# Unread TensorE products in the fox, mlstm and HGRN stages of a two-block kernel, and where these stages begin

## The chip, the cores and the metric

The kernel runs on one core of a Trainium2 chip. TensorE does the matrix products, VectorE, ScalarE and GpSimd the elementwise work, SyncE issues the transfers. The metric is the time of one execution on the device in microseconds; for the kernel before it is the median of three runs. TensorE's clock has two levels in this trace, and the profile gives the granted one as a share of the full 2.4 GHz: 1.00 or 0.50.

## What is computed

Two transformer blocks on 512 tokens of width 1024 in f32. The change touches the second one, whose four mixers (s5, HGRN, fox, mlstm, 256 columns each) stand between an input projection and an output projection. Cut to what matters, and for mlstm and HGRN in the form over all tokens in which the kernel computes them:

```python
# block 2, after block 1 (dilated and latent attention, then an MLP) on x [1, 512, 1024], all f32
qh, kh, vh = heads(q), heads(k), heads(v)              # fox: 4 heads of 64
s = q @ k.T * 64**-0.5 + F[:, None] - F[None, :]       # F = cumsum(log_sigmoid(fz))
s = where(k_pos <= q_pos, s, -1e30)
out = softmax(s) @ v                                   # then a norm by head

# mlstm: q, k = silu(causal 4-tap convolution), gates ig, lf; 4 heads of 64
qk = (q @ k.T) * exp(b[t] - b[s] + ig[s] - m[t]),  s <= t
h = (qk @ v) / max(|sum(qk)|, exp(-m[t]))

# HGRN2: per-channel decays b = cumsum(log f)
scores[t, s] = sum_k q[t,k] * k[s,k] * exp(b[t,k] - b[s,k]),  s <= t
o = scores @ v
# s5: a complex scan, then y = gelu(y) * sigmoid(gelu(y) @ w_glu)
# y = concat(s5, hgrn, fox, mlstm) @ w_out; residual; norm; gated MLP; residual
```

## The kernel before

Tokens lie in four tiles of 128. The program is a row of stages, each an `nc.Block()` with one instruction stream for each engine; a stage's end is a meeting of all engines. Within a stage the engines are ordered by counting semaphores alone, and each engine takes its own instructions in the order of the code. So what stands ahead of an instruction on its engine delays it, whatever it is. PSUM has eight banks, `k.pb[0]` to `k.pb[7]`.

**proj2** (`stage_proj2`) projects the second block's inputs and runs the s5 scan beside it. Its tail is `glu.products`: 24 products of 256 columns into banks 6 and 7, each quarter followed by a sigmoid on ScalarE (`gates`, semaphore `glu.gate`, four counts) and a scaling on VectorE (`scale`).

**fox** (`stage_fox`, which calls `stage_attention`) has 16 batches, four heads by four query tiles; batch i of a head has (i mod 4) + 1 key tiles. TensorE's loop over i runs the scores of batch i, the four or fewer transposes of the probabilities of batch i-1 (`turn`) and the products with the values of batch i-2 (`mix`, 64 columns each). The scores are an f32 product of 64 rows (two instructions in the trace), one of 4 rows for the decays, and a bf16 one with the identity that adds the mask. VectorE takes the maximum, ScalarE the exponential. `Convolution` puts mlstm's convolution on VectorE in iterations 0 to 3 and its sigmoids on ScalarE in iteration 5. The other two attention stages, of the first block, call the same function.

**mlstm** (`stage_mlstm`) also has 16 batches. `scores(b)` makes the logarithms of the decays (2 rows, and the mask) and the f32 scores; ScalarE takes the exponential, VectorE multiplies (`ml_pT`). `scores(b)` waits for the exponential and the product of batch b-2. After the four batches of a head, `mix` of the head before has 20 instructions of 65 columns. `HgrnGates` puts HGRN's gates on VectorE (batches 1, 5 and 10) and on ScalarE (batches 3 and 7).

**HGRN** (`stage_hgrn`) has ten levels (`halves`); at each, VectorE makes operands (`hg_z`, semaphore `zr`), TensorE runs four heads of products into banks 0 to 3, and VectorE selects from them (`sel`). Levels 8 and 9 need a new scan on VectorE. A second block mixes the result with the values while GpSimd and VectorE do the norms of the other mixers; after a third one comes `stage_turn` with transposes, and then the output projection.

Of the kernel before, what the change touches and what calls it, by code (L numbers as in the profile page):

```python
# [30 lines left out]
T = S // P  # L31
# [205 lines left out]
def products(k, out, pairs, first, last):  # L237

    n = 0
    for a, b in pairs:  # L240
        for x, y in ((a.hi, b.hi), (a.hi, b.lo), (a.lo, b.hi)):
            mm = k.nc.tensor.matmul(out, x, y, start=first and n == 0, stop=last and n == 3 * len(pairs) - 1)  # L242
            n += 1
    return mm


def note_freed(k, steps, done):
# [454 lines left out]
        self.free.base += len(self.steps)  # L702


def stage_attention(k, batches, scale, bufs_kb, lse=None, beside=None):

# [19 lines left out]
    with nc.Block() as block:  # L728
# [5 lines left out]
        @block.tensor  # L734
        def _(pe):
            def scores(i):
                b = batches[i]
                if i >= 2:

                    pe.wait_ge(expd.sem, expd.base + i - 1)  # L740
                for (c0, c1), parts in zip(b["segs"], b["scores"]):
                    for m, (a, r, lo, hi, *row) in enumerate(parts):

                        at = dict(tile_position=(row[0], 0)) if row else {}
                        mm = nc.tensor.matmul(k.pb[i % 2][:, lo:hi], a, r, start=m == 0,  # L745
                                              stop=m == len(parts) - 1, skip_group_check=True, **at)
                mm.then_inc(scored.sem, 1)

            def turn(i):
                b = batches[i]  # L750
                pe.wait_ge(expd.sem, expd.base + i + 1)
                if i >= 2:
                    ev = (ev_act, ev_dve)[i % 2]

                    pe.wait_ge(ev.sem, ev.base + i // 2)
                for c in range(0, width(b), P):
                    mm = nc.tensor.transpose(k.pb[2 + i % 2][:, c:c + P], probs[:, i % 2, c:c + P], k.ident[:, :])
                mm.then_inc(turned.sem, 1)

            def mix(i):  # L760
                b = batches[i]
                ev = (ev_act, ev_dve)[i % 2]
                pe.wait_ge(ev.sem, ev.base + i // 2 + 1)
                if i >= 2:

                    pe.wait_ge(out_free.sem, out_free.base + i - 1)
                for n, ((c0, c1), vs) in enumerate(zip(b["segs"], b["values"])):
                    for m, v in enumerate(vs):
                        mm = nc.tensor.matmul(k.pb[4 + i % 2][:, n * DH:(n + 1) * DH],
                                              probsT[:, i % 2, c0 + m * P:c0 + (m + 1) * P], v,  # L770
                                              start=m == 0, stop=m == len(vs) - 1, skip_group_check=True)
                mm.then_inc(mixed.sem, 1)

            for i in range(nb + 2):
                if i < nb:
                    scores(i)
                    if beside is not None:
                        beside.pe(pe, i)
                if 1 <= i <= nb:
                    turn(i - 1)  # L780
                if i >= 2:
                    mix(i - 2)
# [1097 lines left out]
def stage_proj2(k, g):  # L1880
# [15 lines left out]
    for name, _, a, b in PROJ2_FEATURES:  # L1896
        wide = b - a
        tiles = feature_tiles(k.xT, (0, P), wide) if wide == 256 else feature_tiles(k.xT, (0,), wide, m=wide)
        s, j, g = gemm(k, g, KD, 8, tiles, j, BANKS)
# [3 lines left out]
    for c in range(2):  # L1903
        s, j, g = gemm(k, g, KD, 4, token_tiles(lhs, [(0, 512, 0)], 512), j, BANKS)
        steps += s
    s, j, g = gemm(k, g, KD, 8, token_tiles(lhs, [(0, 256, 0)], 256), j, BANKS)
# [6 lines left out]
    rows, glu = GateRows(k), S5Glu(k, end)  # L1913
# [21 lines left out]
    with nc.Block() as block:  # L1935
# [7 lines left out]
        @block.tensor  # L1943
        def _(pe):
            def inject(n):
                q = 32 * (n % 4)
                if n == 0:
                    pe.wait_ge(copied.sem, copied.base + 2)
                else:

                    pe.wait_ge(taken.sem, taken.base + n)
                for c in range(2):
                    mm = nc.tensor.matmul(k.pb[4 + c][:, :], bT[q:q + 32, c, n // 4, :], uT[q:q + 32, n // 4, :],
                                          start=True, stop=True, tile_position=(q, 0))
                mm.then_inc(bu.sem, 1)

            def project(n):
                q = 32 * (n % 4)
                pe.wait_ge(prod.sem, prod.base + n + 1)
                nc.tensor.matmul(k.pb[6 + n // 4][q:q + 32, :], cT[:, 0, n, :], bufs[n % 2][:, 0, :], start=True,  # L1960
                                 stop=False, tile_position=(0, q), skip_group_check=True)
                nc.tensor.matmul(k.pb[6 + n // 4][q:q + 32, :], cT[:, 2, n, :], ei[:, n, :], start=False,
                                 stop=True, tile_position=(0, q), skip_group_check=True).then_inc(out_done.sem, 1)

            seen = set()
            for i, (c, j, out, pairs, start, last) in enumerate(steps):
                if c not in seen:
                    seen.add(c)
                    n = c - first - 2
                    if 0 <= n - 2 < 6:  # L1970
                        project(n - 2)
                    if 0 <= n < 8:
                        inject(n)
                    wait_chunk(k, pe, c)
                if (c, j) == (first + 9, j_tm + 1):
                    project(6)
                if (c, j) == (first + 10, j_tm + T + 2):
                    project(7)
                if (c, j) == (first + 11, j_tm + T + 2):
                    rows.turn(pe)  # L1980
                if j == j_tg + 2:
                    rows.read(pe)
                    glu.turn(pe)
                if start and j >= 4:

                    pe.wait_ge(copied.sem, copied.base + j - 3)
                mm = products(k, out, pairs, start, last)
                if last:
                    mm.then_inc(done.sem, 1)
                elif i in marks:  # L1990
                    mm.then_inc(k.w_used.sem, 1)
            glu.products(pe)

        @block.scalar
        def _(act):
# [318 lines left out]
def stage_fox(k):  # L2314

    batches = []
    for h in range(4):
        lo = DH * (h % 2)
        q, kk = k.fm[lo:lo + DH, 6 + h // 2, :], k.fm[lo:lo + DH, 8 + h // 2, :]
        for t in range(T):  # L2320
# [5 lines left out]
                         (k.identb[:, :], k.mask_row[:, :], t * P, w)]],  # L2326
                values=[[k.tm[:, 2, u, h * DH:(h + 1) * DH] for u in range(t + 1)]],
                out=k.ycat[:, t, 512 + h * DH:512 + (h + 1) * DH]))
    stage_attention(k, batches, 1.0, 158, beside=Convolution(k))


def stage_mlstm(k, hg):
# [12 lines left out]
    with nc.Block() as block:  # L2345
        @block.tensor
        def _(pe):
# [30 lines left out]
            for h in range(5):  # L2378
                if h < 4:
                    for u in range(T):  # L2380
                        scores(4 * h + u)
                if h >= 1:
                    mix(h - 1)

# [117 lines left out]
def stage_hgrn(k, hg):  # L2502
# [20 lines left out]
    with nc.Block() as block:  # L2523
# [81 lines left out]
        def _(pe):  # L2605
            for i in range(nl):
                if i >= 1:
                    pe.wait_ge(zr.sem, zr.base + i)
                for h in range(4):
                    m = 4 * i + h  # L2610
                    if m >= 4:
# [5 lines left out]
                    n = halves[i]  # L2617
# [321 lines left out]
```

## Time and profile before

| | us |
|---|---|
| median of 3 runs | 1773.5 (1773.2 to 1774.2) |
| the profiled execution | 1772.9, of which the span is 1771.1 |
| TensorE busy with products | 1619.4 (91%) |
| VectorE busy | 828.3 (47%) |
| ScalarE busy | 553.8 (31%) |
| mean granted clock of TensorE | 0.92 |
| fox | about 1139.6 to 1200.2 |
| mlstm | about 1200.6 to 1255.6 |
| HGRN, levels | about 1255.9 to 1302.7 |

The span runs from the first to the last instruction; all places in time are microseconds from its start. A line such as `L745` is the line of the code that issued an instruction, and `bank<-fm` says that it wrote a PSUM bank from the tile `fm`; `x4` merges four such instructions in a row. What stands in brackets behind is the engine's idle time before it and what ended that. "Busy" of TensorE is a union of modelled product times, so a busy stretch can hold less array work than it seems.

### The profile page before, as it was taken

How to read it: one execution, taken by the hardware profiler on the slowest of the kernel's cores; microseconds unless marked ns; L12 is line 12 of the kernel's file. 1: busy time of each engine (PE TensorE's matmuls, PEld its weight loads, DVE VectorE, ACT ScalarE, POOL GpSimd, SP SyncE). 2: the span in 40 equal slices, each digit the busy share in tenths (PEclk: the TensorE clock that was granted, in tenths of full speed). 3: DMA queues.
4: the chain of work that ended last, by engine and by line, in shares of the span. 5: the costliest groups of instructions: out<-in, count | busy, mean ns of one | idle time of the engine just before them, and what ended most of it. 6: DMA issues, size and time to landing. Idle time of an engine off the chain costs nothing. (4 is left out here: it accounts for less than half of the span.)

```text
span 1771.1 us, 18376 instructions
## 1 busy us (share of the span) xinstructions
PE 1619.4 (91%) x7372; PEld 1297.5 (73%) x7372; DVE 828.3 (47%) x1217; ACT 553.8 (31%) x839; POOL 261.3 (15%) x275
## 2 busy tenths in 40 slices
PE   7987999678988899999997999999868899999997
PEld 6875777566767788888886766765757688888886
DVE  4233333446654444434336666644664533323434
ACT  4221333424442432222224213334123422212222
POOL 0000000000020697000002466000320100000000
PEclk9999999889998999999998999855759899999999
DMA  4222111220022223222231222200002222222222
GB/s 163 96 92 74 48 48 60 72 72 1 1 71 84 75 102 102 102 97 95 95 119 33 95 72 72 79 0 1 1 1 71 72 95 95 95 95 95 97 85 92
DMA packets 34633, 129.23 MB, mean 73 GB/s; under 512 B 4548, under 2 KB 18780, under 8 KB 22132
## 3 DMA queue, kind: packets, MB, share of 16 engines
q1 hardware_dynamic: 34260, 127.93, 21.1%
q8 instruction: 58, 0.95, 0.2%
q14 instruction: 27, 0.22, 0.0%
q10 hardware_dynamic: 288, 0.12, 0.0%
HBM read 124.82 MB, written 3.17 MB: 72 GB/s over the span
## 5 line engine op out<-in xcount | busy, mean ns | idle before, releaser
L223 DVE TENSOR_TENSOR ring_lo<-ring_raw,ring_hi 128x2048 fp32r<-128x2048 f32 (+5 forms) x115 | 266.7, 2322 | 218.5 <-ACT ring_hi L213 218.4
L242 PE MATMUL bank<-xT_hi,ring_hi 128*128 128x512 f32 (+1 forms) x864 | 342.7, 397 | 5.1 <-PEq L1257 3.4
L242 PE MATMUL bank<-xT_hi,ring_lo 128*128 128x512 f32 (+1 forms) x864 | 338.8, 392 | 0.0
L242 PE MATMUL bank<-xT_lo,ring_hi 128*128 128x512 f32 (+1 forms) x864 | 338.8, 392 | 0.0
L213 ACT CAST ring_hi<-ring_raw 128x2048 fp32r<-128x2048 f32 (+5 forms) x115 | 212.7, 1852 | 270.4 <-DMA ring_raw<-in_w_ff 131.1
L242 PEld LDWEIGHTS bank<-xT_hi,ring_hi 128*128 128x128 f32 (+1 forms) x864 | 163.4, 189 | 44.6 <-issue 10.0
L242 PEld LDWEIGHTS bank<-xT_hi,ring_lo 128*128 128x128 f32 (+1 forms) x864 | 162.8, 188 | 35.6
L242 PEld LDWEIGHTS bank<-xT_lo,ring_hi 128*128 128x128 f32 (+1 forms) x864 | 163.1, 189 | 34.3
L242 PE MATMUL bank<-ring_hi,hid_hi 128*128 128x512 f32 x432 | 169.9, 393 | 4.0 <-DVE ring_lo L223 4.0
L242 PE MATMUL bank<-ring_lo,hid_hi 128*128 128x512 f32 x432 | 169.4, 392 | 0.0
L242 PE MATMUL bank<-ring_hi,hid_lo 128*128 128x512 f32 x432 | 169.3, 392 | 0.0
L1131 POOL TENSOR_TENSOR stat<-stat 128x1 f32<-128x1 f32 x28 | 18.2, 652 | 701.9 <-DVE stat L1172 701.9
L242 PE MATMUL bank<-ring_hi,xT_hi 128*128 128x512 f32 (+1 forms) x288 | 111.5, 387 | 8.9 <-DVE ring_lo L223 8.9
L242 PE MATMUL bank<-ring_hi,xT_lo 128*128 128x512 f32 (+1 forms) x288 | 110.2, 382 | 0.0
L242 PE MATMUL bank<-ring_lo,xT_hi 128*128 128x512 f32 (+1 forms) x288 | 110.1, 382 | 0.0
L242 PEld LDWEIGHTS bank<-ring_hi,hid_hi 128*128 128x128 f32 x432 | 82.1, 190 | 21.4 <-DVE ring_lo L223 4.4
L803 ACT ACTIVATE probs<-bank,nm 128x128 f32<-128x128 f32 (+3 forms) x96 | 50.2, 527 | 148.9 <-DVE nm L829 148.8
L242 PEld LDWEIGHTS bank<-ring_lo,hid_hi 128*128 128x128 f32 x432 | 82.0, 190 | 17.1
L242 PEld LDWEIGHTS bank<-ring_hi,hid_lo 128*128 128x128 f32 x432 | 81.9, 190 | 17.2
L242 PEld LDWEIGHTS bank<-ring_hi,xT_hi 128*128 128x128 f32 x288 | 58.9, 204 | 21.7 <-DVE ring_lo L223 6.5
L827 DVE TENSOR_REDUCE mx<-bank 128x1 f32<-128x512 f32 (+4 forms) x72 | 43.3, 601 | 54.3 <-PE bank L745 54.3
L242 PEld LDWEIGHTS bank<-ring_hi,xT_lo 128*128 128x128 f32 x288 | 58.8, 204 | 9.1
(440 smaller groups left out, 2297.4 us busy)
## 6 DMA issues: line engine op xcount, KB each, us to landing
ring_raw<-in_w_ff SPq DMA_DIRECT2D x32, 1024.0 KB, 4.8
ring_raw<-in_w_up SPq DMA_DIRECT2D x22, 1024.0 KB, 4.9
ring_raw<-in_w_proj SPq DMA_DIRECT2D x8, 1024.0 KB, 5.2
ring_raw<-in_w_gates SPq DMA_DIRECT2D x8, 1024.0 KB, 4.9
ring_raw<-in_w_out SPq DMA_DIRECT2D x8, 1024.0 KB, 4.9
ring_raw<-in_w_fm SPq DMA_DIRECT2D x12, 512.0 KB, 4.5
ring_raw<-in_w_dn_a SPq DMA_DIRECT2D x6, 1024.0 KB, 4.9
ring_raw<-in_w_proj SPq DMA_DIRECT2D x8, 512.0 KB, 4.6
```

Of the source, the lines that this page charges most:

```text
L213: k.nc.scalar.copy(k.ring.hi[:, g % SLOTS, 0:n], k.raw[:, g % SLOTS, 0:n]).then_inc(k.w_hi.sem, 1)
L223: k.nc.vector.tensor_tensor(k.ring.lo[:, g % SLOTS, 0:n], k.raw[:, g % SLOTS, 0:n], plain(k.ring.hi[:, g % SLOTS, 0:n]), ALU.subtract).the ...
L242: mm = k.nc.tensor.matmul(out, x, y, start=first and n == 0, stop=last and n == 3 * len(pairs) - 1)
L803: e = nc.scalar.activation(probs[:, i % 2, c0:c1], k.pb[i % 2][:, c0:c1], ACT.Exp, bias=nm[:, i, n:n + 1], scale=scale, accum_out=ls[:, i, ...
L827: link(nc.vector.tensor_reduce(mx[:, i, 0:m], k.pb[i % 2][:, 0:w].rearrange("p (m w) -> p m w", m=m), AX.X, ALU.max))
L1131: g.tensor_tensor(self.rs[:, x:x + 1], self.ms[:, 16 + x:17 + x], self.half, ALU.pow).then_inc(self.root.sem, 1)
```

## The change

`keep_busy(k, n)` issues n products of the bf16 identity with 512 columns of the bf16 level masks into bank 7; nobody reads them. They carry no semaphore. They stand

- at the end of proj2: ten, behind a new wait of TensorE for the fourth count of `glu.gate`;
- in fox (`busy=2`): eight ahead of the first scores, and two in each of the 18 iterations, between the scores and the transposes;
- in mlstm: two after each of the 16 `scores`;
- in HGRN: three ahead of level 0, six ahead of each of the levels 6, 7, 8 and 9, behind the wait for the level's operands.

The first block's attention stages pass `busy=0` and get none. In all there are 10 + 8 + 36 + 32 + 27 = 113 of them.

```diff
--- before.py
+++ after.py
@@ -242,6 +242,14 @@
             mm = k.nc.tensor.matmul(out, x, y, start=first and n == 0, stop=last and n == 3 * len(pairs) - 1)
             n += 1
     return mm
+
+
+def keep_busy(k, n):
+
+
+    for _ in range(n):
+        k.nc.tensor.matmul(k.pb[7][:, :], k.identb[:, :], k.mask_lev[:, 0:4, :].rearrange("p t s -> p (t s)"),
+                           start=True, stop=True)
 
 
 def note_freed(k, steps, done):
@@ -702,7 +710,7 @@
         self.free.base += len(self.steps)
 
 
-def stage_attention(k, batches, scale, bufs_kb, lse=None, beside=None):
+def stage_attention(k, batches, scale, bufs_kb, lse=None, beside=None, busy=0):
 
 
 
@@ -771,11 +779,14 @@
                                               start=m == 0, stop=m == len(vs) - 1, skip_group_check=True)
                 mm.then_inc(mixed.sem, 1)
 
+            if busy:
+                keep_busy(k, 4 * busy)
             for i in range(nb + 2):
                 if i < nb:
                     scores(i)
                     if beside is not None:
                         beside.pe(pe, i)
+                keep_busy(k, busy)
                 if 1 <= i <= nb:
                     turn(i - 1)
                 if i >= 2:
@@ -1990,6 +2001,8 @@
                 elif i in marks:
                     mm.then_inc(k.w_used.sem, 1)
             glu.products(pe)
+            pe.wait_ge(glu.gate.sem, glu.gate.base + T)
+            keep_busy(k, 10)
 
         @block.scalar
         def _(act):
@@ -2326,7 +2339,7 @@
                          (k.identb[:, :], k.mask_row[:, :], t * P, w)]],
                 values=[[k.tm[:, 2, u, h * DH:(h + 1) * DH] for u in range(t + 1)]],
                 out=k.ycat[:, t, 512 + h * DH:512 + (h + 1) * DH]))
-    stage_attention(k, batches, 1.0, 158, beside=Convolution(k))
+    stage_attention(k, batches, 1.0, 158, beside=Convolution(k), busy=2)
 
 
 def stage_mlstm(k, hg):
@@ -2379,6 +2392,7 @@
                 if h < 4:
                     for u in range(T):
                         scores(4 * h + u)
+                        keep_busy(k, 2)
                 if h >= 1:
                     mix(h - 1)
 
@@ -2606,6 +2620,7 @@
             for i in range(nl):
                 if i >= 1:
                     pe.wait_ge(zr.sem, zr.base + i)
+                keep_busy(k, 3 if i == 0 else 6 if i >= 6 else 0)
                 for h in range(4):
                     m = 4 * i + h
                     if m >= 4:
```

## Rows read from the trace of the kernel before

**Rows 1.** The page's slices of 44.3 us: TensorE's granted clock in tenths.

```profile
PEclk9999999889998999999998999855759899999999
```

**Rows 2.** Busy time by stretches of 10 us; the first line names the columns.

```profile
core 0: us, PE busy (x) PEld busy (x) DVE busy (x) ACT busy (x) POOL busy (x), PEclk, DMA share, GB/s
...
1240.00:1250.00 10.00, 10.00 (x34) 7.03 (x33) 1.95 (x4) 1.42 (x3) 0.00 (x0) 0.50 0.00 0
...
1260.00:1270.00 10.00, 7.47 (x79) 6.99 (x79) 10.00 (x17) 3.18 (x3) 5.92 (x6) 0.97 0.01 2
```

**Rows 3.** Timeline of TensorE in fox: start, us, engine, line, operation, count [idle].

```profile
1152.84 1.12 PE L757 MATMUL bank<-ident,probs 128*128 128x128 f32 x4 [1.20 <-ACT probs L803]
...
1171.55 1.81 PE L769 MATMUL bank<-tm,probsT 128*128 128x64 f32 x8
...
1173.28 1.65 PE L745 MATMUL bank<-fm 64*128 64x384 f32 x2
...
1179.16 0.29 PE L745 MATMUL bank<-mask_row,identb 128*128 128x128 bf16 x1
...
1193.69 0.29 PE L745 MATMUL bank<-mask_row,identb 128*128 128x128 bf16 x1
...
1196.67 3.09 PE L769 MATMUL bank<-tm,probsT 128*128 128x64 f32 x14
```

**Rows 4.** Timeline of VectorE in fox's first head.

```profile
1143.71 0.42 DVE L827 TENSOR_REDUCE mx<-bank 128x1 f32<-128x256 f32 x1
...
1148.48 1.54 DVE L2297 SCALAR_TENSOR_TENSOR conv<-fm,cols,conv 128x511 f32<-128x511 f32 x2
...
1151.11 0.68 DVE L827 TENSOR_REDUCE mx<-bank 128x1 f32<-128x512 f32 x1
```

**Rows 5.** Timeline of mlstm: TensorE behind ScalarE's gates, and its last head.

```profile
1213.80 0.68 PE L2355 MATMUL bank<-m_row,f_right 2*128 2x384 f32 x1 [1.59 <-ACT ml_decay L2393]
...
1237.02 0.79 PE L2355 MATMUL bank<-m_row,f_right 2*128 2x512 f32 x1
...
1245.59 8.79 PE L2374 MATMUL bank<-v_one,ml_pT 128*128 128x65 f32 x40
```

**Rows 6.** Timeline of 512-column products, at clock 1.00 and at 0.50.

```profile
1350.28 0.39 PE L242 MATMUL bank<-ring_hi,ycT_hi 128*128 128x512 f32 x1
1350.51 0.39 PE L242 MATMUL bank<-ring_lo,ycT_hi 128*128 128x512 f32 x1
...
1397.91 0.63 PE L242 MATMUL bank<-xT_hi,ring_hi 128*128 128x512 f32 x1
1398.34 0.63 PE L242 MATMUL bank<-xT_lo,ring_hi 128*128 128x512 f32 x1
```

**Rows 7.** Timeline of the end of proj2 and fox's first product.

```profile
1138.18 0.66 ACT L2146 ACTIVATE s_sg<-bank 128x256 f32<-128x256 f32 x2 [0.78 <-PE bank L242]
...
1139.65 0.46 PE L745 MATMUL bank<-fm 64*128 64x128 f32 x2 [1.51 <-PEq L1935]
```

**Rows 8.** Timeline of the MLA attention stage, at clock 1.00.

```profile
441.34 1.00 PE L769 MATMUL bank<-vB,probsT 128*128 128x64 f32 x8
```

**Rows 9.** Busy time by short stretches, columns as in the second group.

```profile
1141.00:1142.00 1.00, 1.00 (x4) 0.49 (x3) 0.96 (x3) 0.46 (x2) 0.00 (x0) 0.55 0.99 410
1284.00:1286.00 2.00, 0.00 (x0) 0.00 (x0) 1.97 (x3) 0.00 (x0) 0.00 (x0) 0.62 0.00 0
1306.00:1308.00 2.00, 2.00 (x11) 2.00 (x11) 0.71 (x1) 2.00 (x3) 0.00 (x0) 0.50 0.00 0
```

**Rows 10.** Timeline of HGRN: level 0, a scan, level 9, GpSimd's power.

```profile
1255.96 4.92 PE L2625 MATMUL bank<-fm,hg_k 64*128 64x128 f32 x32 [1.58 <-PEq L2345]
...
1283.06 2.29 DVE L2552 TENSOR_TENSOR_SCAN hg_b<-hg_reset,hg_lf 128x1024 f32<-128x1024 f32 x1
...
1297.59 4.02 PE L2625 MATMUL bank<-hg_z 64*128 64x256 f32 x16 [0.38 <-DVE hg_off L2581]
...
1311.60 6.34 POOL L2717 TENSOR_TENSOR fin_rs<-fin_ss,fin_half 128x32 f32<-128x32 f32 x1 [1.58 <-DVE fin_ss L2734]
```

## The prediction

> **What bounds the kernel now.** I read the page's forty slices first: the granted clock is 9 or 1.0 nearly everywhere and 8, 5, 5, 7, 5 in the 26th to 30th, which is where the change works [rows 1]. The tables of busy time by stretch then show what stands there [rows 2, 9]: within 1141 to 1142 the clock falls from 1.00 (the 2.4 GHz level) to 0.50 (1.2 GHz), mean 0.55; at 1240 it is 0.50 as in every ten from 1150 on, with TensorE busy 10.00 of 10 us and VectorE and ScalarE at 1.95 and 1.42. So fox and mlstm run on TensorE at half speed for about 119 us. The timeline shows how tightly: the mask products that end the scores of batches 11 and 15 stand at 1179.16 and 1193.69, 14.53 us for four batches, with nothing but TensorE's own order between them [rows 3]. Two places are not TensorE's. In fox's first four batches VectorE runs the convolution (its two middle steps alone are 1.54 us) between the maxima, and those of batches 1 and 3 stand at 1143.71 and 1151.11, 3.7 us a batch [rows 4], and TensorE waits 1.20 us at 1152.84 [rows 3]. In mlstm ScalarE does HGRN's gates between two decays, and TensorE stands for 1.59 us before 1213.80 [rows 5]. In HGRN VectorE is full (10.00 of 10 us) and TensorE is not (7.47) [rows 2].
>
> **What one unread product costs.** It is a 512-column product on 128 rows. None of this shape in bf16 is in the trace; the nearest are the 512-column products of line 242, 0.23 us from start to start at 1.00 and 0.43 us at 0.50 [rows 6]. From below, only a product in time in which TensorE waits anyway costs nothing. I take 0.23 and 0.43. They write bank 7, which no stage reads while they stand there, so nobody waits for them; what is queued behind them is TensorE's own next instruction.
>
> **The change part by part.** The profiled execution took 1772.9 us (span 1771.1), 0.6 under the median 1773.5.
>
> End of proj2: ten products behind a new wait for the fourth sigmoid, which ends at 1138.84 (1138.18 + 0.66) [rows 7]. Behind them stands the end of the block, and so all engines. Before, fox starts at 1139.65, 0.8 after it, with VectorE's last scaling and the block's end between [rows 7]; now the ten end at 1138.9 + 2.3 = 1141.2, and with 0.4 for the last product's way and the block's end fox starts at about 1141.6: **+1.9**. If the clock were low it would be +3.9, and it cannot be below +1.5.
>
> Head of fox: eight more before the first scores, 8 x 0.23 = **+1.8**. VectorE's chain of the first four batches hangs on those scores and moves as a whole.
>
> Fox, two per batch: in batches 0 to 4 TensorE waits for VectorE anyway (the 1.20 us at 1152.84 covers even 2 x 0.43). From batch 5 on every product is on the path: 0.85 a batch at the low clock, 0.46 at the high one. What the high clock gives back is read from the MLA stage, the same function at 1.00: there 8 mixing products take 1.00 us against 1.81 in fox [rows 3, 8]. So TensorE's work halves.
>
> Where is the clock? It fell at 1141.1 behind the pause 1138.1 to 1139.6 and the short scores after it [rows 7, 9]; the ten and the eight fill that. But then VectorE gives out one batch in 3.7 us, and TensorE's own work for it at the high clock, half of the 3.63 a batch of [rows 3] and less for the short first ones, is some 1.5 us plus 0.46 of filling, about half the time. Behind stretches with such holes the clock falls: in HGRN it falls between 1284 and 1286, where TensorE has nothing (0.00 of 2 us) while VectorE scans [rows 9, 10]. So I expect it to **fall in the first head** in spite of the products. Then it should **rise again inside fox**: it rose just after 1260 behind 4.92 us of back-to-back products [rows 2, 10], and two full products followed by four transposes are, once in four batches, a similar run. It didn't rise without them in 60 us, though TensorE stood busy 10 of 10 us: the mixing products are 64 columns behind a 128-column load, and a stretch of only such ones, busy 2.00 of 2 us at 1306, stayed at 0.50 [rows 9]. I place the rise at batch 10, the middle. Batches 5 to 9: 5 x 0.85 = **+4.3**. From batch 10 (1173.28) to the last product (1199.76) is 26.5 us [rows 3]; halved 13.2, plus 8 x 0.46 = 3.7, is 16.9: **-9.6**.
>
> mlstm: entered at the high clock, batches 0 to 4 run ahead and then wait for ScalarE. ScalarE's stay starts after VectorE's line 2475, which hangs on batch 0's scores; those take 1.2 us less, so batch 5 starts 1.2 us sooner; TensorE has by then stood for some 3 us, and the clock falls as it did at 1284 [rows 9]. After that 11 batches pay 0.85 each, on the path, since TensorE goes through the last head without a gap (1237.02 on: four scores in 8.57 us, then mixing [rows 5]): 9.4 - 1.2 = **+8.2**.
>
> HGRN: the three before level 0 are hidden, VectorE being late anyway [rows 2]. Those of levels 6 to 8 stand in the pauses for VectorE's scans (1283.06, 2.29 us, and so again) [rows 10]. At level 9 TensorE is on the path: six products from 1297.1, then sixteen of 256 columns that took 4.02 us at 0.50 [rows 10]. At the high clock 1.4 + 2.0, about 1.0 sooner; at the low one 2.6 more less 0.5 of waiting, +2.1. I take **-0.5**. The mixing behind it gains nothing: GpSimd's power ends at 1317.94 and VectorE waits for that [rows 10].
>
> Sum: 1.9 + 1.8 + 4.3 - 9.6 + 8.2 - 0.5 = **+6.1**, so 1779.0 for the profiled execution and **1779.6 us** as a median.
>
> **Rivals.**
> *It never rises in fox (the products do nothing but cost).* For it: 60 us of busy TensorE at 0.50. Fox: 1.9 + 1.8 + 13 x 0.85 - 0.4 (one wait for ScalarE hidden) = +14.4. mlstm: 16 x 0.85 = 13.7, less 1.8 in the wait before 1213.80, = +11.9. With -0.5 that is +25.8: **1799 us**.
>
> *It is held high throughout: faster.* Fox from batch 5: 26.5 + 5 x 3.63 = 44.7 us become 22.4 + 13 x 0.46 = 28.4, -16.3, with the +3.7 at its head -12.6. mlstm: the two stays of ScalarE in mlstm set the pace, the last head takes 8.57/2 + 1.8 and two mixings 4.4 us; I get 42 us of 54.9, -13. With -0.5: -26, **1747.5 us**. It decides from the point at which the holes of the first head no longer bring the clock down. For it: HGRN's levels hold the high clock with TensorE busy 7.47 of 10 us [rows 2]. By the Trainium skill (TensorE: Matmul & The Clock Gate, "What's actually happening") the throttled state is the default and activity releases it; by that rule unread products are activity like any others, and this case is what they are for. The trace agrees only in part: fox is busy and stays at 0.50. The same page's "Terms" counts what a low clock costs as the throttled time times one minus the ratio, which for the 110 us from 1150 to 1260 would be 55 us to be had; the rows give 26, since ScalarE and VectorE set the pace at several places.
>
> *Held through fox, lost in mlstm.* -12.6 + 8.2 - 0.5 = -4.9, **1768.6 us**.
>
> **How the numbers follow.** Forecast 0.42 (own range 1772 to 1790, by where in fox the clock rises: at batch 7 it is 8 us less, at batch 14 7 us more), never rises 0.28, held throughout 0.14, held in fox alone 0.16. A time of this kernel can be told from no change from about 0.2% on, 3.5 us. Faster: 0.14 + most of 0.16 = 0.27. Within: the rest of that and the forecast's lower edge, 0.13. Slower 0.60. The range leaves out the case held throughout and little more: 1764 to 1801.
>
> **What would show it.** The granted clock at 1142 to 1150 (1.00 if the ten and eight do their work), at 1150 to 1160 (0.50 if the first head's holes bring it down), and in heads 2 to 4 of fox, where the spacing of the last masks of two heads is 14.5 + 3.4 = 17.9 us at 0.50 and 7.3 + 1.8 = 9.1 us at 1.00. In mlstm the last head's four scores take 8.6 + 3.4 = 12.0 us at 0.50. Wrong would be the forecast if the clock holds 1.00 where TensorE waits for VectorE, or if it stays at 0.50 to the end of fox.

## The result, and the profile after

The changed kernel takes **1793.5 us** (median of four runs, 1792.0 to 1795.2) where the kernel before takes 1773.7 in the same comparison: a ratio of 1.0112, with an interval of 1.0095 to 1.0130. It is 20 us slower; the forecast was 6 us slower, 1779.6 us, in a range of 1764 to 1801.

The page's slices of the kernel after, TensorE's granted clock in tenths; before it read 8, 5, 5, 7, 5 in the 26th to 30th slice [rows 1]:

```profile
PEclk9998999789999999999998999856678899999999
```

The number of unread products can be read from the weight loads, of which each has one (of the products themselves some records are missing). The kernel after, instructions of line 251 by form:

```profile
L251 PEld LDWEIGHTS bank<-mask_lev,identb x113: 95/98/258, 1139.6 to 1319.6; 128*128 128x128 bf16 x113
L251 PE MATMUL bank<-mask_lev,identb x102: 376/379/634, 1139.9 to 1319.8; 128*128 128x512 bf16 x102
```

Busy time of the kernel after by stretches of 10 us, columns as in [rows 2]:

```profile
1140.00:1150.00 10.00, 9.13 (x41) 3.96 (x39) 4.83 (x11) 2.46 (x6) 0.00 (x0) 1.00 0.30 109
1150.00:1160.00 10.00, 6.94 (x30) 4.63 (x31) 9.57 (x22) 1.82 (x5) 0.00 (x0) 0.77 0.00 0
1160.00:1170.00 10.00, 10.00 (x27) 5.12 (x26) 3.39 (x12) 6.60 (x13) 0.00 (x0) 0.50 0.00 0
...
1200.00:1210.00 10.00, 9.78 (x26) 5.12 (x27) 2.98 (x10) 1.82 (x5) 0.00 (x0) 0.50 0.00 0
1210.00:1220.00 10.00, 9.09 (x44) 4.81 (x43) 6.71 (x15) 2.71 (x5) 0.00 (x0) 1.00 0.00 1
1220.00:1230.00 10.00, 7.34 (x18) 2.63 (x18) 4.34 (x10) 6.84 (x10) 0.00 (x0) 0.69 0.01 2
1230.00:1240.00 10.00, 10.00 (x34) 6.55 (x32) 1.98 (x8) 6.93 (x7) 0.00 (x0) 0.50 0.00 0
```

The clock column tells the story. Before, it fell at 1141.1; now the products at proj2's end and ahead of the scores hold it over the stage's start, and it falls at 1155.5. It comes back only at 1210.1, when fox's scores are over, and is lost again at 1223.7, behind the scores of mlstm's first five batches.

The same view in shorter stretches shows what stands around the two falls: ahead of 1155.5 VectorE is nearly full and TensorE is busy 4.66 of 6 us; at 1223.7 ScalarE is.

```profile
1149.00:1155.00 6.00, 4.66 (x22) 2.56 (x23) 5.75 (x11) 1.22 (x5) 0.00 (x0) 1.00 0.00 0
1155.00:1157.00 2.00, 0.16 (x1) 0.00 (x0) 1.89 (x7) 0.51 (x1) 0.00 (x0) 0.62 0.00 0
...
1222.00:1224.00 2.00, 0.56 (x2) 0.11 (x2) 0.00 (x0) 1.98 (x3) 0.00 (x0) 0.94 0.00 0
```

TensorE and ScalarE in the first head of fox, kernel after (timelines, columns as in [rows 3]). In its two lines TensorE waits for the probabilities of a batch, and ScalarE, which makes them, has itself waited 3.59 us for VectorE's maximum. The second wait lasts from 1155.17 to 1157.33, and the clock goes 0.3 us after it has begun; so it cannot be that wait alone; what stands ahead of it counts too (the waits of 0.58 us before 1149.44 and 0.84 before 1152.96, and short products). The transposes behind it are the first products at half speed. Below them, the masks that end the scores of batches 11 and 15, as in [rows 3].

```profile
1152.96 0.55 PE L765 MATMUL bank<-ident,probs 128*128 128x128 f32 x3 [0.84 <-ACT probs L814]
...
1156.49 0.69 ACT L814 ACTIVATE probs<-bank,nm 128x512 f32<-128x512 f32 x1 [3.59 <-DVE nm L840]
...
1157.33 0.90 PE L765 MATMUL bank<-ident,probs 128*128 128x128 f32 x3 [2.16 <-ACT probs L814]
...
1188.76 0.29 PE L753 MATMUL bank<-mask_row,identb 128*128 128x128 bf16 x1
...
1206.71 0.29 PE L753 MATMUL bank<-mask_row,identb 128*128 128x128 bf16 x1
```

The masks stand 17.95 us apart where they stood 14.53 apart [rows 3], 0.85 more a batch. In mlstm and at HGRN's entry (timeline of the kernel after): the wait for ScalarE's decay, 1.59 before [rows 5], is 2.50; two batches of the third head start 3.91 us apart (and so do the same two of the last, 1254.50 and 1258.40); and products stand between mlstm's end and level 0.

```profile
1225.22 0.68 PE L2368 MATMUL bank<-m_row,f_right 2*128 2x384 f32 x1 [2.50 <-ACT ml_decay L2407]
...
1237.90 0.79 PE L2368 MATMUL bank<-m_row,f_right 2*128 2x512 f32 x1
...
1240.85 1.03 PE L251 MATMUL bank<-mask_lev,identb 128*128 128x512 bf16 x2
1241.81 0.68 PE L2368 MATMUL bank<-m_row,f_right 2*128 2x384 f32 x1
...
1277.01 1.01 PE L251 MATMUL bank<-mask_lev,identb 128*128 128x512 bf16 x2 [1.58 <-PEq L2358]
1278.38 2.88 PE L2640 MATMUL bank<-fm,hg_k 64*128 64x128 f32 x17 [0.36 <-issue]
```

The profiled spans differ by 21.0 us (1792.1 less 1771.1). By TensorE's first and last starts in each stage, in both traces, these go:

| part | before | after | difference |
|---|---|---|---|
| from the program's start to the s5 gate's last transposes | 1128.5 | 1129.2 | +0.8, upstream of the change |
| from there to fox's first scores | 11.2 | 14.9 | +3.7 |
| fox, first scores to last mixing | 59.7 | 68.1 | +8.4 |
| to mlstm's first product | 1.3 | 1.2 | -0.1 |
| mlstm, to its last mixing | 53.3 | 61.6 | +8.3 |
| to level 0's first product | 2.0 | 3.4 | +1.4 |
| HGRN's levels | 45.0 | 43.5 | -1.5 |
| the rest | 470.1 | 470.2 | +0.1 |

### The profile page after: what moved, and what is told of

It reads as the page before. It is cut to its first block and busy times, and to the rows that moved or that the text cites. A ratio compares the mean times of both kernels' runs of the same rounds, so it can differ in the third digit from the quotient of the medians.

```text
span 1792.1 us, 18587 instructions
## 1 busy us (share of the span) xinstructions
PE 1641.3 (92%) x7474; PEld 1303.3 (73%) x7485; DVE 829.0 (46%) x1217; ACT 553.8 (31%) x839; POOL 261.2 (15%) x275
```

## The experiments

All are edits of the changed kernel. The same three measures tell each: the time, the stage lengths as in the table above, and the granted clock. The kernel before took 1773.7 to 1774.8 us in the five comparisons; a difference of times is against the one beside it.

| kernel | median us | ratio to before (interval) | fox | mlstm | levels | clock at 0.50, from 1140 to where it next rises behind mlstm |
|---|---|---|---|---|---|---|
| before | 1773.7 | | 59.7 | 53.3 | 45.0 | 1141.1 to 1260.6 |
| changed | 1793.5 | 1.0112 (1.0095 to 1.0130) | 68.1 | 61.6 | 43.5 | 1155.5 to 1210.1, 1223.7 to 1288.6 |
| fox alone | 1784.9 | 1.0062 (1.0047 to 1.0077) | 68.1 | 52.0 | 45.3 | 1157.0 to 1211.6, 1218.4 to 1273.1 |
| mlstm alone | 1787.4 | 1.0075 (1.0060 to 1.0090) | 59.7 | 66.1 | 45.5 | 1141.9 to 1281.9 |
| HGRN alone | 1777.8 | 1.0021 (1.0011 to 1.0031) | 59.7 | 53.3 | 45.1 | 1142.7 to 1269.0 |
| head filled | 1761.8 | 0.9932 (0.9918 to 0.9947) | 45.6 | 52.9 | 45.2 | 1190.1 to 1248.2 |
| four rows | 1804.4 | 1.0170 (1.0154 to 1.0185) | 86.5 | 53.3 | 45.1 | 1142.0 to 1295.6 |
| mlstm held | 1753.7 | 0.9886 (0.9871 to 0.9900) | 45.6 | 43.5 | 45.6 | not in fox or mlstm; 1238.1 to 1248.4 |
| no level 0 | 1796.2 | 1.0126 (1.0109 to 1.0143) | 68.1 | 61.6 | 44.3 | 1156.5 to 1211.1, 1224.8 to 1282.8 |
| grouped | 1784.0 | 1.0056 (1.0041 to 1.0071) | 55.3 | 64.1 | 43.5 | 1148.6 to 1175.9, 1193.0 to 1196.4, 1203.2 to 1278.3 |
| no ten | 1760.6 | 0.9924 (0.9909 to 0.9939) | 48.4 | 52.0 | 45.2 | 1142.5 to 1149.4, 1193.7 to 1248.4 |
| and HGRN | 1753.2 | 0.9881 (0.9867 to 0.9896) | 45.5 | 43.5 | 44.8 | not in fox or mlstm; 1238.6 to 1248.9 |
| stay open | 1777.8 | 1.0020 (1.0011 to 1.0030) | 61.5 | 52.0 | 45.5 | 1165.0 to 1202.6, 1206.0 to 1270.8 |
| changed, dense | 1777.4 | 1.0015 (1.0006 to 1.0024) | 47.1 | 64.1 | 45.1 | 1193.5 to 1268.6 |

The time ahead of the change differs from kernel to kernel by 0 to 2.4 us with the same code in it, and the rest behind HGRN by 2.9 (469.1 to 472.0). So a part of one or two microseconds is read from the stage, not from the end time.

**The parts by themselves.** Three kernels each keep one part. Fox with its two boundaries alone:

```diff
-                        keep_busy(k, 2)
-                keep_busy(k, 3 if i == 0 else 6 if i >= 6 else 0)
```

> Only the products at the end of proj2 and in fox; mlstm and HGRN as before. Theory A (each place has its own price; the clock falls in fox's first head for want of work, comes back only near fox's end, and mlstm's and HGRN's products neither hold nor raise it): fox's last value product ends 11 to 13 us later than before, mlstm is entered high as in the changed kernel and gains 1 to 3 us, HGRN is as before, so 1781 to 1785 us. Rival B (the products of mlstm and HGRN earn their time by holding the clock): without them the kernel is no faster than the changed one, 1793 us or more.

Measured 1784.9 us. Fox takes 68.1 us as in the changed kernel, and mlstm, entered at 1.00 and at 0.50 from 1218.4 on, 1.3 less than before. So fox's part costs 11 us by itself, where the forecast's sum had -1.6 for it with its boundaries.

mlstm alone:

```diff
-            pe.wait_ge(glu.gate.sem, glu.gate.base + T)
-            keep_busy(k, 10)
...
-            if busy:
-                keep_busy(k, 4 * busy)
...
-                keep_busy(k, busy)
...
-                keep_busy(k, 3 if i == 0 else 6 if i >= 6 else 0)
```

> Only the two products after each scores of mlstm. Theory A (they stand on the path at 0.50 and do not raise the clock): 16 x 0.85 = 13.7 less the 1.8 us of waiting ahead of batch 5, +11.9, 1785.6 us, clock 0.50 through all of mlstm. Rival B (they raise it within the stage): the last head's four scores take under 8.6 us, and the kernel is at most 1779 us.

Measured 1787.4 us, 13 over before. The clock never comes up in mlstm. Busy time of this kernel in ten microseconds of it, columns as in [rows 2]:

```profile
1202.00:1212.00 10.00, 10.00 (x19) 3.06 (x18) 4.93 (x10) 3.64 (x6) 0.00 (x0) 0.50 0.00 0
```

Two full products in each batch and TensorE busy 10.00 of 10 us, and 0.50 all the same. mlstm grows by 12.8 us.

HGRN alone keeps the last of the lines above and leaves out the others and mlstm's two per batch.

> Only the products at HGRN's levels 0 and 6 to 9. Theory A: VectorE sets the pace but at level 9, which runs at 1.00 instead of 0.50 and ends about 1 us sooner: 1772 to 1773.5 us. Rival B (level 9 stays at 0.50, the six products are on the path): +2, 1775.7 us.

Measured 1777.8 us, 3.8 over before; 1.6 of the 4.9 that the spans differ lie upstream of any product, 1.8 behind HGRN, and 1.4 at level 0. Timeline of TensorE in this kernel:

```profile
1257.56 1.44 PE L251 MATMUL bank<-mask_lev,identb 128*128 128x512 bf16 x3 [1.58 <-PEq L2353]
1258.93 1.60 PE L2634 MATMUL bank<-fm,hg_k 64*128 64x128 f32 x6
```

The three start where level 0 started before (behind an idle time of 1.58, as in [rows 10]) and level 0 1.37 us later. But the later levels wait for VectorE, which makes its first operands at the same place in both kernels (5.21 us behind mlstm's last mixing), so that level 5 starts only 0.6 us later (23.1 us behind that mixing, 22.5 before). The three cost about 0.6 us and not 1.4.

The levels themselves are no shorter (45.1), so the products of levels 6 to 9 gave nothing here. Level 9 shows why. Timeline of TensorE in this kernel, and in the changed one:

```profile
1299.30 2.42 PE L251 MATMUL bank<-mask_lev,identb 128*128 128x512 bf16 x6 [0.47 <-DVE hg_z L2576]
```

```profile
1318.75 1.47 PE L251 MATMUL bank<-mask_lev,identb 128*128 128x512 bf16 x6 [0.47 <-DVE hg_z L2582]
1320.14 2.10 PE L2640 MATMUL bank<-hg_z 64*128 64x256 f32 x16
```

In this kernel the clock is at 0.50 from 1299.7 to 1303.1, just there, and the six take 2.42 us; in the changed one it is at 1.00, the six take 1.47 and the sixteen of level 9 2.10, against 4.02 before [rows 10]. So what level 9 gains hangs on where the low stretches of the clock fall among the levels.

**The first iterations denser.** The theory was that the number of products is not what fails, but where they stand: fox's first head is where VectorE leaves holes.

```diff
-            if busy:
-                keep_busy(k, 4 * busy)
...
-                keep_busy(k, busy)
+                keep_busy(k, (6 if i < 5 else 5 if i < 8 else 1) if busy else 0)
```

and none in mlstm and HGRN.

> The ten at the end of proj2, none ahead of fox's first scores, and in fox six in each of iterations 0 to 4, five in 5 to 7, one in each later one; none in mlstm and HGRN. Theory A (the clock falls for want of array work while VectorE does the convolution and ScalarE its sigmoids, and products put exactly there hold it): 1.00 through all of fox; from batch 5 on the 44.7 us become 22.4 plus 15 + 10 products x 0.23, so about 28; with +1.9 at proj2's end, -13 to -15 at the end of fox, and mlstm 1 to 3 us shorter for being entered high: 1757 to 1762 us. Rival B (unread products do not hold the clock; it falls anyway within the first head): the 25 products from batch 5 on cost 0.43 each and the thirty before them up to 5 us more than the waits hide: +12 to +18, 1786 to 1792 us.

Measured 1761.8 us: 12 us faster than the kernel before, with 65 unread products instead of 113. Busy time of this kernel, and below it the same 10 us more of fox:

```profile
1140.00:1150.00 10.00, 9.51 (x42) 4.29 (x43) 6.64 (x14) 2.59 (x7) 0.00 (x0) 1.00 0.36 137
1150.00:1160.00 10.00, 10.00 (x57) 6.26 (x56) 9.58 (x24) 2.28 (x7) 0.00 (x0) 1.00 0.00 0
...
1170.00:1180.00 10.00, 10.00 (x59) 6.70 (x58) 7.75 (x25) 2.99 (x10) 0.00 (x0) 1.00 0.01 2
```

VectorE is as full as in the changed kernel (9.58 against 9.57), TensorE now too, and the clock stays at 1.00 to 1190.1, through all of fox, which takes 45.6 us. It goes at mlstm's entry. By the Trainium skill (TensorE: Matmul & The Clock Gate, "What's actually happening") activity releases the throttle; this kernel agrees, and the changed one shows that activity of a sort is there without it: 9.78 to 10.00 busy and 0.50.

**What the activity has to be.** The same kernel with each unread product reading 4 rows instead of 128:

```diff
-        k.nc.tensor.matmul(k.pb[7][:, :], k.identb[:, :], k.mask_lev[:, 0:4, :].rearrange("p t s -> p (t s)"),
+        k.nc.tensor.matmul(k.pb[7][:, :], k.identb[0:4, :], k.mask_lev[0:4, 0:4, :].rearrange("p t s -> p (t s)"),
```

> The kernel with the head of fox filled (ten products at the end of proj2, none ahead of the first scores, in fox six in each of iterations 0 to 4, five in 5 to 7, one in each later one, none in mlstm and HGRN), which took 1761.8 us, with one thing changed: each unread product reads 4 rows of the array instead of 128. It has the same 512 columns. Theory A: what keeps the granted clock at 1.00 is work in the array, which a product of 4 rows hardly is; then the clock falls within the first ten us of fox as in the kernel before, the products cost 0.43 us each and give nothing back: fox gets 1.9 us later start, up to (15 + 8) x 0.43 = 9.9 us from batch 5 on and some 2 to 5 us before it, 1785 to 1791 us. Theory B: a TensorE that is busy is enough; then the clock stays at 1.00 through fox and the time is again 1760 to 1764 us.

Measured 1804.4 us, 43 over the same kernel with 128 rows, and more than either theory's number. TensorE's timeline in this kernel, then its busy time from 1165 to 1180, and last the same stretch of the kernel with 128 rows:

```profile
1139.88 2.38 PE L251 MATMUL bank<-mask_lev,identb 4*128 4x512 bf16 x10 [0.75 <-ACT s_sg L2157]
1142.56 0.77 PE L753 MATMUL bank<-fm 64*128 64x128 f32 x2 [0.30 <-PEq L1944]
...
1143.87 2.74 PE L251 MATMUL bank<-mask_lev,identb 4*128 4x512 bf16 x6
```

```profile
1165.00:1180.00 15.00, 15.00 (x44) 7.86 (x44) 3.03 (x11) 5.44 (x11) 0.00 (x0) 0.50 0.00 0
```

```profile
1165.00:1180.00 15.00, 14.57 (x87) 9.85 (x85) 10.45 (x32) 5.99 (x18) 0.00 (x0) 1.00 0.00 1
```

The ten at proj2's end take their 0.23 us each, no idle time of TensorE over 0.30 us stands anywhere in fox, and the clock falls at 1142.0 and stays down to 1295.6. Ahead of the fall TensorE was as busy as in the kernel with 128 rows, whose clock did not fall there. The four us up to it, and the same stretch of the other kernel:

```profile
1138.00:1142.00 4.00, 3.25 (x20) 1.78 (x18) 1.50 (x4) 1.05 (x4) 0.00 (x0) 1.00 0.94 350
```

```profile
1138.30:1142.30 4.00, 3.25 (x20) 1.82 (x18) 1.51 (x4) 1.05 (x4) 0.00 (x0) 1.00 0.94 352
```

So it is not that TensorE has something to do; what the product does in the array counts. Whether it is the rows, or the data in them (the 128 rows of the identity hold 128 ones, the 4 rows four), this run doesn't tell. Both theories' numbers were too low because few of the products at 0.50 find a wait to lie in: with six of 0.43 us a batch takes TensorE 4.5 to 6.6 us from mask to mask in the first head, where VectorE gave out one in 3.7 [rows 4], so that fox pays from batch 1 on (86.5 us).

**How the same number stands.** In fox eight in every fourth iteration (32) instead of two in each (36); all else as changed.

```diff
-                keep_busy(k, busy)
+                keep_busy(k, (8 if i % 4 == 3 else 0) if busy else 0)
```

> The changed kernel with about the same number of unread products in fox, put otherwise: eight in every fourth iteration (behind the scores of batches 3, 7, 11 and 15, 32 in all) instead of two in each of eighteen (36). Theory A: it is not their number but the length of an unbroken run of full products that brings the clock up; eight of them with the widest transposes behind them do so once a head, so that the clock rises at batch 4 to 8 instead of at the end of fox: fox some 12 to 16 us shorter, 1778 to 1783 us. Theory B: the number counts: the clock rises at the end of fox again, 1791 to 1794 us.

Measured 1784.0 us, and fox 12.8 us shorter than in the changed kernel. Timeline and busy time of this kernel where the second eight stand:

```profile
1171.56 3.19 PE L251 MATMUL bank<-mask_lev,identb 128*128 128x512 bf16 x7 [0.22 <-issue]
```

```profile
1174.00:1176.00 2.00, 2.00 (x9) 1.62 (x7) 0.00 (x0) 0.48 (x1) 0.00 (x0) 0.51 0.00 0
1176.00:1178.00 2.00, 2.00 (x16) 1.70 (x15) 1.27 (x4) 0.46 (x2) 0.00 (x0) 1.00 0.00 0
```

Right behind them the clock rises, at 1175.9, in batch 7 of 16; two in each iteration took to the end of the stage. At 1.00 batches 8 to 15 then take 2.3 us each with only the groups of 11 and 15 to help, and the clock stays up to 1193.0. The eight behind batch 3's scores (1153) had not raised it, so a run of eight does it in one place and not in another; what more it takes is open. (A third run stands behind batch 15's scores: the clock, lost at 1193.0, is back at 1196.4.) The end time is 1 us over the expected range, because mlstm takes 64.1 us here and not 61.6: it loses the clock at 1203.2, 2.6 us in.

**The second hole.** The kernel with the head filled, with one product instead of five in iterations 5 to 7, where ScalarE leaves the softmax for the convolution's sigmoids:

```diff
-                keep_busy(k, (6 if i < 5 else 5 if i < 8 else 1) if busy else 0)
+                keep_busy(k, (6 if i < 5 else 1) if busy else 0)
```

> The kernel with the head of fox filled, with one product instead of five in iterations 5 to 7, where ScalarE leaves the softmax for the convolution's sigmoids; 12 products fewer, 2.8 us at 1.00, of which those in waits give nothing. Theory A: with VectorE's convolution over, TensorE's own work is dense enough and the clock stays at 1.00 (in the filled kernel TensorE waited for ScalarE there only 0.43 us); up to 2 us less: 1760 to 1762 us. Theory B: ScalarE's stay is a second hole, the clock falls at 1160 to 1168 and stays at 0.50 to the end of fox, some 20 us at half speed: 1770 to 1780 us.

Measured 1777.8 us: twelve products fewer, 2.8 us of work at 1.00, cost 16 us. Timeline and busy time of this kernel:

```profile
1165.20 0.90 PE L765 MATMUL bank<-ident,probs 128*128 128x128 f32 x3 [2.21 <-ACT probs L812]
```

```profile
1162.00:1165.00 3.00, 0.99 (x4) 0.29 (x3) 0.96 (x4) 2.97 (x6) 0.00 (x0) 1.00 0.00 0
1165.00:1170.00 5.00, 4.80 (x20) 4.14 (x21) 1.22 (x4) 1.76 (x7) 0.00 (x0) 0.50 0.00 0
```

ScalarE is full (2.97 of 3), TensorE stands for 2.21 us, and behind that fox goes at 0.50 to its end. The clock falls at 1165.0, when the wait has lasted 2.0 us. The first head's hole, which is filled here, no longer brings it down, and this one by itself does.

**The boundary.** The kernel with the head filled, without the ten at proj2's end and their wait:

```diff
-            pe.wait_ge(glu.gate.sem, glu.gate.base + T)
-            keep_busy(k, 10)
```

> The kernel with the head of fox filled (1761.8 us, 0.9932 of before) without the ten products at the end of proj2 and without their wait. Theory A: the ten are needed, since TensorE otherwise has next to nothing from the last tiles of proj2 to the first scores; then the clock falls at 1141 to 1150, the six products in each of the first iterations cost 0.43 us, and it comes back up only later in fox, as with groups of eight (27 us of low clock, some 8 us dearer): 1764 to 1772 us. Theory B: the six behind each of the first scores are enough to hold 1.00 by themselves; then their 1.5 us at the head are saved: 1760 to 1761 us.

Measured 1760.6 us, in B's range, but by A's mechanism. Busy time of this kernel:

```profile
1140.00:1150.00 10.00, 8.93 (x24) 3.62 (x24) 7.06 (x14) 2.83 (x7) 0.00 (x0) 0.66 0.37 138
1150.00:1160.00 10.00, 10.00 (x55) 5.98 (x55) 8.52 (x20) 2.07 (x6) 0.00 (x0) 1.00 0.00 0
```

The clock does fall, at 1142.5, and is back at 1149.4 behind the sixes of iterations 0 and 1. Fox takes 2.8 us more and starts 1.9 us earlier. The intervals of the two kernels overlap: where dense products follow, the ten neither pay nor cost.

**mlstm.** The kernel with the head filled, and mlstm filled by its own holes, 70 products:

```diff
+                    if h == 0:
+                        keep_busy(k, 7)
                     for u in range(T):
                         scores(4 * h + u)
-                        keep_busy(k, 2)
+                        keep_busy(k, (10, 0, 5, 5, 7, 9, 2, 2, 8, 4, 1, 5, 2, 3, 0, 0)[4 * h + u])
```

> The same filled fox (128 rows), and mlstm filled where TensorE waits there: seven products ahead of its first scores and 10, 0, 5, 5, 7, 9, 2, 2, 8, 4, 1, 5, 2, 3, 0, 0 behind those of its sixteen batches, none in HGRN. Theory A: mlstm falls to 0.50 only because TensorE stands for VectorE's and ScalarE's work at its entry and in ScalarE's stays; filled there the clock stays at 1.00, and mlstm takes 45 to 50 us instead of the 52.9 of the kernel with fox alone filled: 1753 to 1760 us. Theory B: mlstm loses the clock all the same, in its own short products; then 70 products at 0.43 us, of which some 10 us lie in waits, make it some 15 to 20 us longer: 1777 to 1782 us.

Measured 1753.7 us: 21 us faster than the kernel before in the same comparison. mlstm takes 43.5 us, 9.8 less than before. Busy time of this kernel in mlstm, with the stretch in which ScalarE makes HGRN's gates:

```profile
1197.00:1207.00 10.00, 9.95 (x39) 4.17 (x40) 3.73 (x11) 7.61 (x10) 0.00 (x0) 1.00 0.00 0
```

The slices of the page, same kernel: the 26th to 28th, 8, 5 and 5 before [rows 1], are full.

```profile
PEclk9999999888998999999999999999859999999999
```

The 9.8 us are not all won: the seven products ahead of mlstm's first scores put these off by 1.5 us (they start 2.8 us behind fox's last mixing, 1.3 before).

With HGRN's six ahead of each of levels 6 to 9 added to it (none at level 0):

> The kernel with fox and mlstm filled (1753.7 us) and six products ahead of each of HGRN's levels 6 to 9, as in the changed kernel, without those of level 0. Theory A: the products of levels 6 to 8 lie in TensorE's waits for VectorE's scans and keep the clock up; at level 9 TensorE is on the path, and six products at 1.00 cost 1.4 us and give 2.0 back; 0 to 2 us less: 1751.5 to 1754 us. Theory B: they cost more than they give, as in the kernel with HGRN's products alone (levels 1258.9 to 1304.1, no shorter than before): 1755 to 1757 us.

Measured 1753.2 us, the same within the intervals; the levels are 0.7 us shorter. These products give nothing that the end shows.

**Level 0.** The changed kernel without its three:

```diff
-                keep_busy(k, 3 if i == 0 else 6 if i >= 6 else 0)
+                keep_busy(k, 6 if i >= 6 else 0)
```

> The changed kernel without the three products ahead of HGRN's level 0, all else as it is (1793.5 us). Theory A: they stand on the path, as the kernel with HGRN's products alone suggests (it lost 3.8 us, and its level 0 started 1.4 us behind the mixing instead of 2.0 us with 1.4 us of products between): 1792.0 to 1792.4 us. Theory B: they are hidden behind VectorE, as forecast, and the 3.8 us come from somewhere else: 1793.5 us.

Measured 1796.2 us. Timeline of this kernel at HGRN's entry:

```profile
1274.73 1.70 PE L2387 MATMUL bank<-v_one,ml_pT 128*128 128x65 f32 x7
1278.01 2.21 PE L2640 MATMUL bank<-fm,hg_k 64*128 64x128 f32 x12 [1.58 <-PEq L2358]
```

Level 0 starts 2.0 us behind mlstm's last mixing again, 1.4 sooner than in the changed kernel, as A has it, but the levels take 0.8 us more, since those behind level 0 keep to VectorE's pace: level 5 starts 22.5 us behind the mixing, as before the change, and 23.1 in the changed kernel. So the three are worth 0.6 us to the levels. The end time doesn't show it: 1 us more lies upstream, 1 us more in the rest.

**The changed kernel with a dense head.** Only fox's first eight iterations differ, six and five products instead of two, and the eight ahead of the scores are gone. It is the forecast's rival "held through fox, lost in mlstm".

```diff
-            if busy:
-                keep_busy(k, 4 * busy)
...
-                keep_busy(k, busy)
+                keep_busy(k, (6 if i < 5 else 5 if i < 8 else 2) if busy else 0)
```

> The changed kernel with one thing other: its unread products in fox's first eight iterations are six (0 to 4) and five (5 to 7) instead of two, and the eight ahead of the first scores are gone; two per iteration from the eighth on, two per batch in mlstm, and HGRN's, all as in the changed kernel. It is the forecast's rival held in fox, lost in mlstm (1768.6 us). Theory A: 29 more unread products in the first eight iterations hold the clock at 1.00 through fox, which the changed kernel loses at 1155.5; fox as in the filled kernel (1761.8) plus 9 to 10 products of 0.23 us, mlstm's two per batch at a high entry cost 8.3 us as measured in the changed kernel, HGRN adds nothing or takes 1 off: 1769 to 1773 us. Theory B: it is the eight ahead of the scores or the later iterations' count that matter, the clock falls again in the first head: over 1790 us.

Measured 1777.4 us, 16 us faster than the changed kernel, though it issues 21 products more. Fox is held to its end (47.1 us), as A has it. But mlstm takes 64.1 us, not 61.6. Busy time of this kernel at mlstm's entry:

```profile
1190.00:1193.00 3.00, 2.09 (x7) 0.69 (x6) 1.21 (x4) 0.69 (x1) 0.00 (x0) 1.00 0.03 8
1193.00:1195.00 2.00, 2.00 (x6) 0.79 (x4) 2.00 (x5) 0.58 (x1) 0.00 (x0) 0.63 0.00 0
```

It loses the clock at 1193.5, 2.5 us in, where the changed kernel kept it for 10 us with the same instructions. What two per batch cost in mlstm goes by how long the clock lasts there: against the 53.3 us of the kernel before, 8.3 us where it went 10.3 us in, 10.8 and 10.8 where it went 2.6 and 2.5 in, 12.8 where it was never up.

## Why the prediction was right, and where it was not

The sign and the range held, and so did the terms for the boundary, the head and mlstm, and for HGRN as a sum. The size was 14 us short, and nearly all of that is one step, the rise of the clock inside fox. That 1793.5 lies in the range at all is owed to the range's width: it was drawn to take in the rival "it never rises", while the forecast's own range, 1772 to 1790, was missed, and the rival's 1799 is nearer than its own 1779.6. What the kernel did is that rival in fox and the forecast in mlstm.

- **Boundary and head of fox**: +3.7 forecast (1.9 and 1.8), +3.7 measured, with the clock at 1.00 over them as forecast. Fox's first scores in the dense kernel, which has only the ten, start 1.9 us later than before once the upstream 1.2 is taken off.
- **The fall in the first head**: forecast "in spite of the products", and it came at 1155.5, where VectorE is busy 5.75 of the 6 us ahead and TensorE 4.66. The kernel with the head filled and the changed one with a dense head show that this hole is the cause: in both it is filled and the clock passes it. The one with the stay open shows that ScalarE's is a second of its kind, which the forecast did not list.
- **The price at 0.50**: 0.85 a batch and 17.9 us between the masks of two heads; measured 17.95. In mlstm a batch costs up to 0.97 (3.91 less 2.94 from the batch's start to the next, before 1237.02 to 1239.97), so that the last head's four scores take 12.3 us (1254.50 to 1266.79) rather than 12.0.
- **The rise inside fox: this step failed.** The forecast took it at batch 10, the middle, from "two full products followed by four transposes are, once in four batches, a similar run" to HGRN's 4.92 us of back-to-back products [rows 10]. It came at 1210.1, behind the last scores. So all of batches 4 to 15 paid (the masks of 4 and 15 stand 52.2 us apart, 42.3 before: +9.9, where eleven batches at the rival's 0.85 make 9.4), and the -9.6 behind the rise never came. Forecast for fox itself +4.3 - 9.6 = -5.3, measured +8.4: that is 13.7 of the 14.9 us by which the profiled spans miss the forecast's +6.1; the rest is spread over the time upstream, HGRN and the others. The own range reached to batch 14. The prediction named as a sign of being wrong that the clock "stays at 0.50 to the end of fox"; it did, but for the last 2 us of the stage, in which only transposes and mixing are left. For fox the rival "it never rises" had the mechanism right, at +10.7 without the head where 8.4 were measured. The grouped kernel shows how far off the likeness was: two full products in each iteration did not raise the clock in mid-fox in any of the three kernels that have them there at 0.50, and even of the runs of eight the one at 1153 did not and the one at 1171.56 did.
- **mlstm**: +8.2 forecast, +8.3 measured, entered at 1.00 and lost at ScalarE's stay (2.50 us of idle time) as described; batch 5 starts 1.3 us sooner behind mlstm's start (1.2 forecast), and what follows takes 9.6 us more (9.4 forecast). That it was entered at 1.00 is in part luck: the forecast had the clock up from the middle of fox, and it came up 3.3 us ahead of mlstm's first product. And the number holds for this entry only: 2.5 us dearer where the clock goes at once.
- **HGRN**: -0.5 forecast, and -0.1 measured. That the three ahead of level 0 are hidden, "VectorE being late anyway", is right for 0.8 of their 1.4 us. They put level 0 itself off by 1.4 us in all four kernels that have them, since it waits for nothing of VectorE and the idle time ahead of it is of TensorE's own sequencer (`PEq`); the levels behind it wait for VectorE and come 0.6 us later. Level 9 at 1.00 gave 0.7 us, where the forecast had about 1.0, and only where the clock was up at that place.

The rival "held high throughout" was given 1747.5 us. It did not happen here, but its sizes can be set beside kernels in which the clock is held: for fox 16.3 us less than before, which is 43.4, where the dense kernel with 29 products more in it takes 47.1; for mlstm 13 less, where the kernel that holds it takes 9.8 less and gives 1.5 of that back at the entry; and 1753.7 us in all. The rival "held through fox, lost in mlstm", 1768.6, can be set beside the dense kernel, 1777.4. In the profiled spans it is 9.4 us dearer than that rival: 3.7 in fox with its 29 products, 2.6 in mlstm, 2.0 at level 0 and in the levels, and 1.8 behind HGRN, where no edit stands, less 0.7 at the starts of fox and mlstm.

## What to carry to other kernels

In this kernel, products that nobody reads paid only where they closed a hole in front of a stretch long enough to gain from the higher clock, with about as many as the hole takes. Spread evenly over a stretch in which TensorE is the bound at 0.50 already, they were a plain cost for each; a run of eight at 0.50 raised the clock in two places of three. Whether the single products in the later iterations of the kernels with the head filled are needed was not tested. First list the places where another engine makes TensorE wait within such a stretch, since one left open (2.2 us here) gave back what all the others had won. Then read the granted clock over the whole stretch, not at its start.

## What was not expected of the hardware

- Occupied and active are two things: with 4 rows a product, TensorE is busy 15.00 of 15 us at 0.50; with 128 rows, 14.57 of 15 at 1.00, and 43 us lie between the two kernels.
- The time doesn't go by the number of such products at all: 113 give 1793.5 us, 65 give 1761.8, 134 give 1777.4 and 135 give 1753.7, by where they stand.
- A lost clock can be back within 7 us (1142.5 to 1149.4) or take 55 (1155.5 to 1210.1) in the same stage, by what follows it.
- mlstm entered at 1.00 with the same instructions keeps the clock for 10.3 us in one kernel and 2.5 in two others. The instructions up to the earlier fall are the same. What differs is the moment of the entry, and what stood ahead of it: in the first the clock had risen 3.3 us before the entry, in one of the others 4.2, and in the third it had been up through fox. Which of these decides is open, since no run moved one alone.
